# A two-layer decoder step on one core: a planner's rules for the order of three engines, and the places of the first bulk loads

## The reference

```python
def layer(x, ...):
    proj = rmsnorm(x, norm1) @ w_in            # 1024 x 2568: q, k, v, o, pooled inputs, gates
    hm = mLSTM over (q, k, v, gates), normed, times sigmoid(o)
    zp = pooled trailing windows of u_pool, times w_pool
    x = x + concat(hm, zp) @ w_out             # 1024 x 1024
    x = x + peer_ffn(rmsnorm(x, norm2), ...)
    x = x + sigmoid(x @ w_gate) * (p @ w_ple)  # 1024 x 1024, 256 x 1024

def peer_ffn(xb, wq, keys, u_tab, v_tab):
    q = (xb @ wq).reshape(T, 8, 2, 128)        # 1024 x 2048
    s = einsum('thcd,chkd->thck', q, keys)
    sv, si = top_k(s, 16)                      # per head, both halves
    cand = sv[:, :, 0, :, None] + sv[:, :, 1, None, :]
    top, sel = top_k(cand, 16)
    eidx, gate = the 16 experts of each head, softmax(top)
    act = gelu(einsum('td,thkd->thk', xb, u_tab[eidx]))
    return einsum('thk,thkd->td', gate * act, v_tab[eidx])
```

## Time and profile before

| what | value |
|---|---|
| median of 3 runs | 1766.37 us (1765.01 to 1769.4) |
| the profiled execution | 1755.1 us, span 1753.0 us |
| granted TensorE clock, mean | 0.830 of full speed |
| busy: PE, DVE, ACT, POOL | 77%, 57%, 39%, 29% of the span |
| DMA | 687.26 MB, 392 GB/s over the span, of them 553.68 MB by the gathers |

### The profile page before, as it was taken

How to read it: one execution, slowest core, us unless ns; L and a number is a source line. 1 busy time by engine, 2 the same in 40 slices (tenths; PEclk the granted TensorE clock), 3 DMA queues, 4 the chain that set the end, 5 groups by cost and what they waited for, 6 DMA issues and landing times. The chain is left out here.

```text
span 1753.0 us, 19301 instructions
## 1 busy us (share of the span) xinstructions
PE 1352.5 (77%) x6310; PEld 496.6 (28%) x6310; DVE 997.0 (57%) x2540; ACT 689.7 (39%) x1963; POOL 501.0 (29%) x532
## 2 busy tenths in 40 slices
PE   7888987887668888667677997798666857676766
PEld 4443433343113343211112443343311211111113
DVE  1277668568744355964445434848964434455544
ACT  3146444333435353243333635443443433333334
POOL 0022223222332022243333212222343233333330
PEclk9988988999769999986658898999876875677669
DMA  8599999999999999989999999999999989999993
GB/s 320 192 381 374 409 395 423 386 389 370 381 427 427 378 422 399 388 364 427 427 426 426 426 375 419 418 414 411 368 393 427 427 356 427 427 428 427 427 427 158
DMA packets 96737, 687.26 MB, mean 392 GB/s; under 512 B 11104, under 2 KB 12640, under 8 KB 14318
## 3 DMA queue, kind: packets, MB, share of 16 engines
q0 software_dynamic: 76032, 553.68, 76.4%
q1 hardware_dynamic: 20606, 132.36, 18.7%
HBM read 679.87 MB, written 6.59 MB: 392 GB/s over the span
## 5 line engine op out<-in xcount | busy, mean ns | idle before, releaser
L2125 DVE SCALAR_TENSOR_TENSOR rows<-rows,shown 128x1024 f32<-128x1024 f32 x528 | 638.8, 1221 | 600.5 <-DMA rows<-in_uv,index_B 325.2
L1259 PE MATMUL acc<-rows,weighted 128*64 128x512 f32 x2048 | 695.7, 784 | 232.5 <-ACT weighted L1650 222.7
L1456 POOL DMA_INDIRECT rows<-in_uv,index_A x256 | 243.1, 950 | 683.3 <-PE acc L1259 537.2
L946 PE MATMUL bank<-wring,turned 128*128 128x512 f32 (+1 forms) x840 | 385.9, 607 | 18.3 <-DMA wring<-in_w 18.0
L1456 POOL DMA_INDIRECT rows<-in_uv,index_B x256 | 242.7, 948 | 501.6 <-PE acc L1259 482.4
L1259 PEld LDWEIGHTS acc<-rows,weighted 128*64 128x64 f32 x2048 | 134.7, 161 | 710.7 <-ACT weighted L1650 585.1
L946 PEld LDWEIGHTS bank<-wring,turned 128*128 128x128 f32 x840 | 158.2, 196 | 201.9 <-issue 178.4
L1639 ACT ACTIVATE dots_B<-dots_B 128x1 f32<-128x1 f32 x256 | 51.7, 202 | 361.6 <-DVE rows L2125 359.3
L1639 ACT ACTIVATE dots_A<-dots_A 128x1 f32<-128x1 f32 x256 | 51.2, 200 | 327.4 <-DVE rows L2125 317.7
L1650 ACT ACTIVATE weighted<-consts,dots_A 128x64 f32<-128x64 f32 x256 | 89.0, 348 | 8.4
L1650 ACT ACTIVATE weighted<-consts,dots_B 128x64 f32<-128x64 f32 x256 | 89.0, 348 | 8.4
(11 more groups left out here) (312 smaller groups left out, 986.9 us busy)
## 6 DMA issues: line engine op xcount, KB each, us to landing
wring<-in_w SPq DMA_DIRECT2D x107, 1024.0 KB
out_sample<-scratch SPq DMA_DIRECT2D x2, 2128.5 KB
scratch<-in_c_s SPq DMA_DIRECT2D x2, 2064.0 KB
rows<-in_uv,index_A POOLq DMA_INDIRECT x256
rows<-in_uv,index_B POOLq DMA_INDIRECT x256
keys<-in_keys SPq DMA_DIRECT2D x2, 1024.0 KB
gain<-in_gain SPq DMA_DIRECT2D x3, 640.0 KB
consts<-in_consts SPq DMA_DIRECT2D x1, 1243.0 KB, 10.9
```

What stands on the lines that cost most here:

```text
L946: ins = pe.matmul(ps[:, part], turned["A"][:, 4 * h + c, :], w[:, c, part], start=first, stop=end, skip_group_check=True)
L1259: ins = pe.matmul(acc[c * 64:(c + 1) * 64, :], weighted[:, n % STATS, :], row[:, c * BLOCK:(c + 1) * BLOCK], start=first, stop=end, skip_g ...
L1456: pool.indirect_dma_start(out=rows[:, n % RING, :], out_offset=None, in_=a["uv"], in_offset=bass.IndirectOffsetOnAxis(ap=index[kind][:, pa ...
L2125: dve.scalar_tensor_tensor(u, u, 1.0, shown[:, :, :], ALU.mult, ALU.mult, accum_out=dots[kind][:, part, i:i + 1]).then_inc(u_used, 1)
```

## The change

The scheduler's rules and costs change, and with them the order in which PE, DVE, ACT and SP do the same work. `RUNWAY` becomes 12 us for PE and 15 us for ACT and DVE. Stages "project", "gates" and "query" no longer need "norm" before their first step, only before the later ones (`scale_of`). A step of ACT that needs another table of functions counts as beginning `TABLE` = 1.3 us later when candidates are compared (`reload`). A gather that reaches an idle stream costs 2.75 us in the plan instead of 2.47. Some costs change by a few per cent. The show of tile 0 moves from ahead of the first query to behind the first turn_index, the second half of its query 1 behind the first turn_prob, and the bulk loads of layer 0 to three places during the projections. The closing stages of the sample tile 5 become a line of their own.

```diff
         early = [("query", 0, FIRST, h, big) for h in range(2)]
-        early += [("turn_pq", big, FIRST), ("match", big, FIRST)] + [("query", 0, 1, h, big) for h in range(2)]
-        out = [e for e in out if e not in early]
+        early += [("turn_pq", big, FIRST), ("match", big, FIRST), ("query", 0, 1, 0, big)]
+        after = [("show", big, 0), ("query", 0, 1, 1, big)]
+        out = [e for e in out if e not in early + after]
         at = out.index(("rank", big, 0, 2))
         out[at:at] = early
+        at = out.index(("turn_index", big, 0, 1)) + 1
+        out[at:at] = after[:1]
+        at = out.index(("turn_prob", big, 0, 1)) + 1
+        out[at:at] = after[1:]
...
-    "project": (("PE", 3.4), ("ACT", 0.7)), "cum": (("PE", 0.4), ("DVE", 1.1)), "spread": (("PE", 0.9), ("DVE", 1.7)),
+    "project": (("PE", 3.55), ("ACT", 0.7)), "cum": (("PE", 0.4), ("DVE", 1.1)), "spread": (("PE", 0.9), ("DVE", 1.7)),
...
+THIN, SPARSE = 2.0, 2.75
...
-AHEAD, RUNWAY = 8, 7.0
+AHEAD, RUNWAY = 8, {"PE": 12.0, "ACT": 15.0, "DVE": 15.0}
...
-            self.dma = max(self.dma, self.pool + FLIGHT) + ROW
+            self.dma = max(self.dma, self.pool + FLIGHT) + (ROW if self.dma > self.pool + FLIGHT + THIN else SPARSE)
...
+    def reload(self, engine, e):
+
+        table = table_of(e) if engine == "ACT" else None
+        return TABLE if table and table != self.table else 0.0
+
+    def scale_of(self, e):
+
+        t = tile_of(e)
+        if e[0] in ("project", "gates"):
+            return self.finish_of(("norm", t, "turn"))
+        if e[0] == "query":
+            return self.finish_of(("norm", t, "turn2"))
+        if e[0] in ("turn", "turn2", "final") and KIND[t] != "S":
+            n = self.norms.index(("norm", t, e[0]))
+            return self.finish_of(self.norms[n - 1]) if n else 0.0
+        return 0.0
...
-                dry = self.dma - self.at[engine] < RUNWAY
+                dry = self.dma - self.at[engine] < RUNWAY[engine]
...
-                        found.append((max(at, self.at[engine]), self.rank_of(line, head[0], short, dry), line, head))
+                        found.append((max(at, self.at[engine]) + self.reload(engine, head[0]), self.rank_of(line, head[0], short, dry), line, head))
...
+    last = [e for e in closing if e[0] != "embed" and tile_of(e) == PASS_TILES[LAST][-1]]
+    closing = [e for e in closing if e not in last]
     for part in (others, third, fourth, closing):
         lines.append(Line([e for e in part if e not in silent], tuple(lines[1:])))
+    lines.append(Line(last, lines[-1].after))
...
+            def load_pool(layer):
+                sp.dma_start(gain2[:, :], a["gain"][layer]).then_inc(layer_in, 16)
+                sp.dma_start(w_pool[:, :, :].rearrange("p g n -> p (g n)"), a["w_pool"][layer]).then_inc(layer_in, 16)
+
+            def load_keys(layer):
+                sp.dma_start(keys[:, :, :].rearrange("p a b -> p (a b)"), a["keys"][layer]).then_inc(layer_in, 16)
...
-                    sp.dma_start(keys[:, :, :].rearrange("p a b -> p (a b)"), a["keys"][layer]).then_inc(layer_in, 16)
-                    sp.dma_start(gain2[:, :], a["gain"][layer]).then_inc(layer_in, 16)
-                    sp.dma_start(w_pool[:, :, :].rearrange("p g n -> p (g n)"), a["w_pool"][layer]).then_inc(layer_in, 16)
-                    if layer == 0:
-                        load_tiles()
+                    if layer:
+                        load_pool(layer)
+                        load_keys(layer)
+                if e == ("project", 0, 1, 1, 0):
+                    load_pool(0)
+                if e == ("project", 0, 2, 1, 0):
+                    load_keys(0)
+                if e == ("project", 0, 4, 0, 0):
+                    load_tiles()
```

## The result

| | before | changed |
|---|---|---|
| median of the runs on one chip | 1767.01 us (1765.01 to 1769.4) | 1695.66 us (1691.82 to 1699.47) |
| the profiled execution | 1755.1 us, span 1753.0 | 1699.47 us, span 1697.3 |
| first gather issued | 98.68 | 86.31 |

The ratio is 0.9596, 95% interval 0.957 to 0.9621: the change gains 71 us between the medians. The forecast was 1734.4 in a range of 1718 to 1755; faster was right, the size was not.

A forecast was written before the change was run, and what follows sets the result against it. The prediction took the kernel to be bound by the DMA stream, gaining only where it stands idle: start 10, stream 20 and tail 2 make 32 us, so 1766.4 - 32 = 1734.4 us, in a range of 1718 to 1755.

The forecast's parts named there:

- The start: Ahead of the first gather: issue moves from 98.7 to 86.3; gain 10 us, bounds 7 and 11.
- the three steps named: PE before the first gather: no weights wait (4.6 us), show moved away (5.1), half of query 1 moved (2.7); together 12.4.
- the second step: Without the show and PE's wait for xn ahead of it, the first query begins at 73.7, not 78.80: 5.1 us.
- The stream's idle time: Gathers' stream: longer runway lets consumers catch up before long steps; gain 20 us, 15 of it in rankings, bounds 0 and 42.
- the other 5 us: Part of the stream's 20 us: from dense runs on PE and the small gaps of the stream.
- The failed step: Whole stream: the lower DMA rate while engines are busy was held untouched by the change, so no gain was counted.
- the three terms of the sum: Gains forecast for the start (10 us), the stream (20 us) and the tail (2 us), together 32 us.
- The tail: After the last rows: tile 5's gate products start 4.4 us earlier, last sigmoid waits for ACT; gain 2 us, bounds 0 and 4.4.
- The gaps stay: Rival: only start and tail pay, 12 us, giving 1754.4 us; chance 0.2.
- nothing: Rival: gaps in the stream grow by what the start gives, as new stalls replace the old; 1766 us, chance 0.05.
- Nearly every gap goes: Rival: all stream gaps but the 6.2 us at 1410 vanish; gain 54 us, 1712.4 us, chance 0.13.
- Too late: Rival: consumers first delays the dense chain, so PE waits for `chosen`; slower, 1772 us with 67 us of lateness, chance 0.05.

The follow-up runs named there:

- E2: Kernel before plus only the rule that a normed product waits for its own norm (scale_of), runway still 7.0: 1773.71 us, ratio 1.006.
- E1: Kernel before plus RUNWAY 12/15/15 us and the rule that a normed product waits for its own norm; start and costs old: 1708.17 us, 0.969.
- E5: Changed kernel with RUNWAY back at 7.0 us for all three engines, all else kept: 1749.58 us, ratio 0.9947.
- E9: Changed kernel, lists unchanged, but SBUF holds 6 rows of gathers instead of 8: 1787.41 us, ratio 1.0145.
- E12: Changed kernel with the last tile's closing steps in one line with the others again: 1696.26 us, ratio 0.9617.
- E4: Kernel before with only SP's bulk loads spread over three places, every list as before: 1760.21 us, ratio 0.9982.
- E11: Changed kernel with RUNWAY 18 us for all three engines: 1725.7 us, ratio 0.9792.
- E16: Changed kernel with ACT's order no longer counting a change of table as a later begin: 1693.46 us, ratio 0.9611.
- E7: Changed kernel with the planner's old costs and no dearer row in a thin stream: 1685.77 us, ratio 0.9587.
- E14: The changed kernel with the planner's old costs, run again on another chip: 1684.17 us, ratio 0.9557.
- E8: Changed kernel without the rule that a normed product waits for its own norm: 1689.36 us, ratio 0.9606.

## Why the prediction was right in direction and short in size

**The start: right mechanism, the exact figure in part luck.** Forecast first gather 86.3, measured 86.31, by the three steps named. But the steps were not each as forecast: the transposes behind the mix begin 3.5 us earlier (4.6 forecast), the first query another 5.9 (5.1), the first turn_index another 3.0 (2.7), and the errors cancel. Part of the second step is the rule's: E2 has 3.4 us less between the transposes and turn_index without the new start. Idle start is 11.5 us less, against a gain taken as 10.

**The stream's idle time: right mechanism, slightly small.** I took 20 us with bounds 0 and 42; the trace shows 24.8. The rankings' gaps are gone, as forecast: by the shares some 17 of their 18.6 us, for 15. The dense run of tiles 1 and 2, from which part of the other 5 us was to come, gave nothing (4.0 us idle for 4.3), so the rest came from small gaps. The wait for `emb` stays (10.62 for 10.53 us), as forecast. E1, E2 and E5 show that it is the runway.

**The failed step** is the sentence "The rest of the distance to 1613 is a lower rate while the engines are busy, which nothing in the change touches." The lower rate was a second price of the thin ring: 28.6 of the 40.2 us of excess were in packets of gathers, 26.9 of them in those with at most two gathers behind. The change took 15.1 us of the excess. That the runway does it, E2 to E1 and the changed kernel to E5 show on either base (24.6 and 16.4 us), and E9 moves it without any change of list. Between the two profiled executions 23.7 us were missing from the forecast of 32: these 15.1, together 7.9 by which the three terms of the sum were too small, and 0.7 in the rest. I could have seen it: the queue's share on the page, times the span, gives 1339 us for 553.68 MB, which is 413 GB/s. The undisturbed stream had 426 at a share of 1.01, which is 422 at 1.

**The tail: right mechanism, too small.** Forecast 2 with bounds 0 and 4.4; the two profiled executions show 3.6 and E12 4.1. The samples' last sigmoid waits for ACT as forecast (no idle on ACT from 1686.55 to 1690.93). But the forecast kept the samples' products at their old pace, 3.84 us from `turned_s` to the first sigmoid. It is 2.17 us, as PE, which stood 0.99 us and not 5.34, did them at a granted clock of 1.00 for 0.58. That is the missing 1.6.

**The rest, 16 us, is where the profiled executions lie.** 32 us were counted on a profile of 1755.1 us and taken from a median of 1766.4. E4, with the lists of before, idled 7.5 us longer in its stream and had 6.2 us more excess than the profile of before. A remedy for idling is worth more on the median run than on such a good one; by how much, a single trace can't say. That this makes up the whole 16 us is argued, not shown, and E4's trace is a single one.

**The rivals.** "The gaps stay" and "nothing" are refuted by E5 against the changed kernel. "Nearly every gap goes" (1712.4, 0.13) came nearest; it deserved more, since the rankings' gaps were certain to go and it had the reason (the long stretches between them ran full). "Too late" did not happen in this list, but E11 shows that the same rule with 18 us runs into it, at the two changes of tile where POOL waits for index_B; I had looked at that of tile 4 alone.

**Table loads, costs, rule.** I forecast nothing of the first and left the others out of the sum; E16, E7, E14 and E8 show no gain from any that can be measured. The Trainium skill, DMA: Bandwidth & Descriptors, section Queues, rings and completion order, has each DMA engine take turns between rings that have work. By it the loads of weights would be slower with a fuller ring of gathers. The trace agrees with the turns: 128 packets of a half of weights took 4.5 us among 108 of gathers, and the 256 small ones of `emb` 5.2 us among 248. Together they are nearly the whole wait of 10.62 us for `emb`, which both kernels have. What the trace does not bear out is more waiting for weights with a fuller ring: over the stream PE waits for weights 10.5 us in 3 waits, less than the 14.6 in 5 of the earlier trace rows:

```profile
PE bank L982 <- DMA wring<-in_w: 10.5, 3, 5.0
```

## What to carry to other kernels

Where a stream of gathers is the bound, count its time in two parts: idle time, and the duration of its packets against their duration when the ring is full. A thin ring costs both, so what fills the ring pays more than the gaps show: here 60% more, and 50% where the runway alone was changed (E2 to E1, changed to E5). Try a rule that puts consumers first at several strengths, and look at every change of tile for what the chain behind must deliver: too little starves the ring in the long steps (7 us of runway: 0.995), too much makes the next indices late (18 us: 0.979); with 15 to 16.5 us for DVE and ACT and the new start it was 0.956 to 0.962. Look also at what stands ahead of a small load in its queue: a half of weights and the gathers' turns made 160 KB wait 10 us. And before taking a profile's gaps from a median, look how far the profiled execution lies from it.

## What the runs showed of the hardware

A packet of 8 KB of a gather takes 309 to 314 ns on the mean with three or four gathers queued behind it, 320 to 323 with one, and 325 to 342 with none (before, changed, E9), with the same rows, sizes and engines. The median is 309 ns throughout: it is a few packets that take long (1037 over 400 ns before, 543 changed, 1551 in E9, of 67584), with none queued behind most of all the first 16 of a gather. Over one execution the excess of all packets came to 21.6 us in E14 and 52.4 in E9, and nearly two fifths of that of before (15.1 of 40.2) went by the order of the work and the places of loads alone.

Beside a filled ring of gathers a plain load gets about every second packet, whatever the sizes: 256 packets of 640 bytes took 5.2 us among 248 of 8 KB, though one of them takes 32 ns.
